# The first head's queries (and, in one layer, its pair's keys) computed ahead of the inverse transform in the second block

## What is computed

```python
def mla_queries(p, q_norm_g, w_uq, rope):
    cq = rms_norm(p[..., OFF_Q:OFF_KV], q_norm_g)
    q = (cq @ w_uq).reshape(B, L, MLA_HEADS, QK_NOPE + QK_ROPE)
    ...                                   # the last 32 channels of a head are rotated (rope)
def mla_attention(q_nope, q_rope, k_nope, k_rope, v):
    s = (jnp.einsum('bqhd,bkhd->bhqk', qn, k_nope) + jnp.einsum('bqhr,bkr->bhqk', qr, k_rope))
    prob = jax.nn.softmax(s.astype(jnp.float32) * scale, axis=-1).astype(v.dtype)
...
att_x = mla_attention(qn_x, qr_x, concat([kn_x, kn_c]), concat([kr_x, kr_c]), concat([v_x, v_c]))
x = x + g1 * heads_out(att_x, px, hy, w_out[l])      # attention, Fourier mix and hyena, side by side, by w_out
```

## The kernel before

| | values | back | first queries |
|---|---|---|---|
| layer 0 | v3 on 4, v4 on 5, v5 on 4 | c: 6 and 7 | 4, then 5, 6, 7 |
| layer 1 | v3 on 4, v4 on 5, v5 on 6 | x: 0 and 1 | 4, then 5 |

## Times and profile before

### The profile page before, as it was taken

How to read it: one execution, slowest core, us unless ns; L and a number is a source line. 1 busy time by engine, 2 the same in 40 slices (tenths; PEclk the granted TensorE clock), 3 DMA queues, 4 the chain that set the end, 5 groups by cost and what they waited for, 6 DMA issues and landing times.

```text
span 2508.6 us, 30040 instructions
## 1 busy us (share of the span) xinstructions
PE 2390.9 (95%) x11574; PEld 1858.9 (74%) x11574; DVE 1426.5 (57%) x2243; ACT 907.1 (36%) x1543; POOL 565.5 (23%) x431
## 2 busy tenths in 40 slices
PE   6999999999999997888999999999999989999998
PEld 5665667888877874667888888888775567788886
DVE  4465546888757436665475565544636674533435
ACT  4244444223244223675332221222421773423222
POOL 2523114223121213002131211211223002322221
PEclk9999899999999999999999999999999999999999
DMA  5411114555521311001144444331122112222321
GB/s 184 151 55 43 54 35 166 194 185 184 185 80 43 107 64 57 20 26 46 38 137 132 128 131 133 120 105 57 49 97 76 34 35 68 86 91 93 104 89 52
DMA packets 77913, 234.05 MB, mean 93 GB/s; under 512 B 9343, under 2 KB 12416, under 8 KB 77772
## 3 DMA queue, kind: packets, MB, share of 16 engines
q1 hardware_dynamic: 70928, 217.48, 26.4%
q0 software_dynamic: 3520, 11.58, 1.4%
q10 hardware_dynamic: 3324, 3.08, 0.4%
HBM read 224.20 MB, written 7.90 MB: 93 GB/s over the span
## 4 chain that ended last, share of the span: by engine, by line
PE 86%; DVE 7%; ACT 3%; issue 2%; POOL 2%; ACTq 0%; DVEq 0%; POOLq 0%
PE psum L652 35%; PE psum L923 24%; PE psum L691 4%; PE psum L1225 3%; PE psum L635 3%; PE psum L1256 2%; PE psum L1182 2%; PE psum L711 2%; PE psum L828 1%; PE psum L799 1%; PE psum L1240 1%; PE psum L577 1%; DVE mla_stat L2035 1%; PE psum L1196 1%; PE psum L846 1%
## 5 line engine op out<-in xcount | busy, mean ns | idle before, releaser
L652 PE MATMUL psum<-mix_split,weight_split 128*128 128x512 f32 (+1 forms) x3456 | 708.8, 366 | 1.3 <-POOL weight_split L2657 1.0
L652 PEld LDWEIGHTS psum<-mix_split,weight_split 128*128 128x128 f32 x3456 | 589.4, 188 | 117.4 <-POOL weight_split L2657 1.4
L923 PE MATMUL psum<-hidden,weight_split 128*128 128x512 f32 (+1 forms) x3072 | 629.5, 366 | 0.0
L923 PEld LDWEIGHTS psum<-hidden,weight_split 128*128 128x128 f32 x3072 | 523.7, 188 | 102.4
L2113 ACT CAST weight_split<-weight_ring 128x1024 fp32r<-128x1024 f32 x269 | 277.1, 1041 | 298.4 <-PE psum L923 231.6
L2657 POOL TENSOR_TENSOR weight_split<-weight_ring,weight_split 128x1024 fp32r<-128x1024 f32 x89 | 234.6, 2636 | 536.7 <-ACT weight_split L2113 536.2
L1681 DVE TENSOR_TENSOR hidden<-hidden_tmp,hidden 128x512 fp32r<-128x512 f32 (+1 forms) x128 | 157.1, 1247 | 313.8 <-POOL hidden_tmp L2790 313.8
L2790 POOL TENSOR_TENSOR hidden_tmp<-hidden_tmp 128x512 f32<-128x512 f32 (+1 forms) x128 | 126.3, 998 | 608.9 <-ACT hidden L2367 608.8
L1319 DVE TENSOR_TENSOR weight_split<-weight_ring,weight_split 128x1024 fp32r<-128x1024 f32 x180 | 228.5, 1272 | 51.7 <-ACT weight_split L2113 51.7
L2363 ACT ACTIVATE hidden_tmp<-psum 128x512 f32<-128x512 f32 (+1 forms) x128 | 69.2, 541 | 491.3 <-PE psum L652 491.3
L1698 DVE SCALAR_TENSOR_TENSOR residual<-psum,modulation,residual 128x512 f32<-128x512 f32 x192 | 120.0, 657 | 157.6 <-PE psum L923 157.6
(11 more groups left out here) (309 smaller groups left out, 2656.8 us busy)
## 6 DMA issues: line engine op xcount, KB each, us to landing
weight_ring<-in_w_mlp SPq DMA_DIRECT2D x128, 512.0 KB, 3.9
weight_ring<-in_w_ff SPq DMA_DIRECT2D x64, 512.0 KB, 4.8
mod_ring<-in_w_mod SPq DMA_DIRECT2D x48, 512.0 KB, 3.9
late_ring<-in_w_mod SPq DMA_DIRECT2D x96, 256.0 KB, 3.6
weight_ring<-in_w_in SPq DMA_DIRECT2D x45, 512.0 KB, 3.8
weight_ring<-in_w_out SPq DMA_DIRECT2D x24, 512.0 KB, 3.7
weight_ring<-in_tables SPq DMA_DIRECT2D x13, 512.0 KB, 3.6
weight_ring<-in_w_v SPq DMA_DIRECT2D x8, 512.0 KB, 4.3
```

The source lines that it names most:

```text
L652: m = pe.matmul(psum[:, b + r, 0:hi - lo], w[:, part_w, :], x[:, part_x, k, lo:hi], start=k == 0 and part_w + part_x == 0, stop=k == KT - ...
L923: mm = pe.matmul(psum[:, b + r, 0:hi - lo], w[:, part_w, :], G[:, part_x, f % (2 * GROUP), lo:hi], start=jj == 0 and part_w + part_x == 0, ...
```

## The change

`make_pair` on PE moves out of `attention_2` and becomes a generator that is begun in `mid`. A new helper `first_head` takes its first steps: in layer 0 four of them (queries of head 0 in two ranges, keys of the pair in two ranges), between values 5 and back c; in layer 1 one (queries of head 0), inside back x between f = 0 and f = 1. `attention_2` takes the rest; for the first pair the order is now queries, keys, queries, on all engines. Pairs 1 to 3 keep their order. On DVE the two products of the rotation (new helper `rope_products`) of head 0 go ahead of the convolution's last four instructions; the sum stays behind `hyena`. The last `back` of a layer takes its two banks from the pool "logits". ACT gets an activation of one column (exp of a constant, whose result nothing reads) ahead of its wait for `hyena`, and with it the load of its function table. The loads of w_uq and w_uk move ahead of the inverse table.

```diff
+            def make_pair(l, p):
+                tag, RG = f"mla{l}", ranges_of(l)
+                def queries(h, i):
...
+                i, i_k = use_load("w_uq", (l, p), 2 * 3 * P), use_load("w_uk", (l, p), 2 * P)
...
+                pe.wait_ge(*landed(i))
+                for part in (queries(2 * p, i), keys(), queries(2 * p + 1, i)) if p == 0 else (queries(2 * p, i), queries(2 * p + 1, i), keys()):
+                    yield from part
...
+                def first_head():
+                    pe.wait_ge(*when(f"qn{l}_vec", ("scaled", 2, len(RG) - 1)))
+                    first_pair[l] = make_pair(l, 0)
+                    for _ in range(1 if l else 4):
+                        next(first_pair[l])
                 def back(lo, hi, nm):
-                    b = take(2)
+                    b = take(2, "logits") if (lo, hi, nm) == streams[-1] else take(2)
                     for f in range(n):
+                        if l and f:
+                            first_head()
...
                     make_values([5])
+                    first_head()
                     back(*streams[1])
...
-                for _ in make_pair(0):
+                for _ in first_pair[l]:
                     pass
...  (vector_program)
+                    if (lo, hi, nm) == streams[-1]:
+                        rope_products(l, 0)
                     ve.wait_ge(*when("table", bank_of[tag, "back_load", nm]))
...  (scalar_program, attention_2)
+                ac.activation(rs[:, 0:1], vec("eps"), ACT.Exp).then_inc(*did("table_act", tag))
                 ac.wait_ge(*when(f"mid{l}_vec", ("hyena", streams_of(l)[-1][2], 1)))
```

More of the change, by code:

```diff
@@ L1171, in attention_2 @@
                 pe.wait_ge(*when(f"mid{l}_vec", ("v", 5)))
[L1173 to L1196, removed]
-                        m.then_inc(*did(tag + "_pe", ("k", p, r)))
-                        freed[b] = [(tag + "_act", ("k", p, r)), (tag + "_vec", ("k", p, r))]
-                        if r == 1:
-                            done_with[i] = (tag + "_pe", ("k", p, 1))
-                        yield
                 def logits(n):
@@ L2008, in make_pair, with keys @@
                             yield
[L2009 to L2015 removed]
+                    def keys():
+                        for r, (lo, hi) in enumerate(XB):
+                            h = 2 * p
+                            ve.wait_ge(*when(tag + "_pe", ("k", p, r)))
+                            if h > 2:
+                                ve.wait_ge(*when(tag + "_pe", ("logits", last_logits[h - 3])))
+                            ve.tensor_copy(KH[0:64, h % 3, lo:hi], psum[0:64, bank_of[tag, "k", p, r], 0:hi - lo]).then_inc(*did(tag + "_vec", ("k", p, r)))
+                            yield
+                    for part in (queries(2 * p), keys(), queries(2 * p + 1)) if p == 0 else (queries(2 * p), queries(2 * p + 1), keys()):
+                        yield from part
                 def feed(n):
@@ L2554, in make_pair, with keys @@
                             yield
-                    for r, (lo, hi) in enumerate(XB):
-                        h = 2 * p + 1
-                        ac.wait_ge(*when(tag + "_pe", ("k", p, r)))
-                        ac.wait_ge(*when(tag + "_vec", ("k", p, r)))
-                        if h > 2:
-                            ac.wait_ge(*when(tag + "_pe", ("logits", last_logits[h - 3])))
-                        ac.copy(KH[0:64, h % 3, lo:hi], psum[64:128, bank_of[tag, "k", p, r], 0:hi - lo]).then_inc(*did(tag + "_act", ("k", p, r)))
-                        yield
+                    def keys():
+                        for r, (lo, hi) in enumerate(XB):
+                            h = 2 * p + 1
+                            ac.wait_ge(*when(tag + "_pe", ("k", p, r)))
+                            ac.wait_ge(*when(tag + "_vec", ("k", p, r)))
+                            if h > 2:
+                                ac.wait_ge(*when(tag + "_pe", ("logits", last_logits[h - 3])))
+                            ac.copy(KH[0:64, h % 3, lo:hi], psum[64:128, bank_of[tag, "k", p, r], 0:hi - lo]).then_inc(*did(tag + "_act", ("k", p, r)))
+                            yield
+                    for part in (queries(2 * p), keys(), queries(2 * p + 1)) if p == 0 else (queries(2 * p), queries(2 * p + 1), keys()):
+                        yield from part
                 def feed(n):
```

55 lines of the change are left out of this document (37 added, 18 removed).

## The result

The changed kernel takes 2510.18 us (median of 20 runs, 2508.19 to 2514.2), the kernel before 2506.48 in the same comparison (20 runs, 2502.98 to 2511.09). The ratio is 1.0015, 95% interval 1.0010 to 1.0021: 3.7 us slower, inside what I called the same. The profiled execution took 2514.2 us with a span of 2512.4, against 2508.6 before, at the same mean clock of 0.981.

The account below looks back on a forecast made before the run. PE, busy 95% of the span, bounds the kernel, so moves pay only where it idles. Layer 0's -0.4 and layer 1's +3.3 sum to +2.9 us; from the median 2507.27 that gives 2510.2 us, range 2507.5 to 2512.3.

Parts of the forecast that it names:

- what I called the same: Whole kernel: differences below about 0.2%, 5.0 us, count as no change; chance of same 0.81.
- layer 0, queries start: Layer 0 on PE: moved queries wait for DVE's subtraction of value 5, start about 971.95; the gap stays.
- layer 0, convolution starts: Layer 0 on DVE: convolution follows back c's last start at 982.3 by 0.25, at 982.55.
- layer 0, logits: Layer 0, start of attention: first logits at 987.2, 0.4 us earlier.
- layer 1, back x starts: Layer 1 on PE: back x's first half waits for value 4's subtraction, starts 1932.1 after 7.3 us idle.
- layer 1, clock's cost behind the gap: Layer 1, back x and moved matmuls: lowered clock behind the gap costs 2.1 us.
- layer 1, first maximum: Layer 1, start of softmax: first logits 3.2 us later, another 0.1 from DVE's head 1 rotation, +3.3.
- layer 1, fall at the softmax: Layer 1, start of softmax: the likeliest case keeps the clock's fall, a loss of some 1.7 us.
- The step that failed: Layer 0 on PE: second head's queries end at 986.4, in time for logits at 987.2.
- the second rival: Layer 1, start of softmax: the clock's fall of some 1.7 us goes away; +1.2, 2508.5 us, chance 0.25.
- two terms that the prediction had at 0: Layer 0's attention and what follows it up to layer 1: no change in either, 0 us.
- The rival on the slower side: Layer 1's back x loses another 2.1 to the clock, layer 0's softmax start 1.7: +6.7, 2514.0 us, chance 0.13.

Follow-up runs that it names:

- The pool alone: Kernel before, only change: the last back stream alone draws its banks from the logits pool, nothing moved; 2511.36 us, ratio 1.0009.
- the free banks: Changed kernel, same order, with fixed free banks for first pair and last back: layer 0 2498.71 us, layer 1 2501.04, both 2491.66.
- other banks: Changed kernel with layer 0's second-head queries on banks 2 and 3 and first logits starting on bank 0; 2508.70 us, ratio 1.0006.
- before's second trace: Kernel before, profiled once more with no change; one run, span 2503.4 us.
- free banks in layer 1: Changed kernel with fixed free banks in layer 1 only, 2501.04 us, or in both layers, 2491.66 us.
- layer 1 alone: Changed kernel, but layer 0's queries and keys stay behind back c in the new first-pair order; 2506.27 us, ratio 0.9991.
- order alone: Kernel before with only the first pair reordered and the early table load, nothing moved ahead of back; 2508.91 us, run again 2509.97.
- layer 0 alone: Changed kernel, but layer 1's queries stay behind back x in the new first-pair order; 2509.69 us, ratio 1.0009.
- the two second traces: Kernel before and changed kernel, each profiled once more unedited; one run each, spans 2503.4 and 2506.5 us.
- both layers' banks: Changed kernel with fixed free banks in both layers for the first pair and last back; 2491.66 us, ratio 0.9939.

## Why the prediction came out right, step by step

| step | predicted | trace of the change |
|---|---|---|
| layer 0, queries start | 971.95 after 7.2 idle | 971.87 after 7.30, released by DVE's value 5 |
| layer 0, convolution starts | 982.55 | 982.64 |
| layer 0, logits | 987.2 (-0.4) | 989.13 (+1.5; L0 +1.24) |
| layer 1, back x starts | 1932.1 after 7.3 | 1932.1 after 7.11, less layer 0's shift |
| layer 1, clock's cost behind the gap | 2.1 | 2.7 (6.35 for 3.62) |
| layer 1, first maximum | +3.3 | +3.97 |
| layer 1, fall at the softmax | stays | gone, att -1.67 |
| sum | +2.9 | +3.7 timed, +3.8 span |

The mechanism held but for one wait: both gaps stay because the bank decides, and most of the loss is the first half of back x moved behind DVE's values. The pool alone shows that part by itself, and the free banks show that nothing else kept the gaps open.

**The step that failed** is "The second head's queries end on PE at 982.3 + 3.87 + 0.2 = 986.4, in time." I had followed the banks to the first moved matmul and to back, and not to the third user of the ring. Head 1's queries draw bank 4 again, which holds head 0's queries. Its last reader is ACT's copy (984.47 to 985.05), which waits for hyena, and hyena now comes after back c. So PE stood idle for 2.59 us, the queries ran until 989.3, and the first logits, next in PE's list, came at 989.13 instead of 987.2. With other banks the term is -0.5, as summed. The error is 1.6 to 1.8 us.

**Sizes.** The clock's cost in layer 1 was 0.6 short in this trace and 0.3 too high for the second (5.42 - 3.62 = 1.8); it varies over runs of the same kernel. On the other side 1.67 came back at the start of layer 1's softmax, which is the term of the second rival (1.7). But it is no clear gift of the change: before's second trace has no fall there, and has one of 1.7 later, between the 21st and 22nd maximum of layer 1; its L1 att is 131.00 all the same. Both traces of before have one fall in layer 1's attention up to there; the six traces with more than 7 us of idle time before back x have none, and neither have the two with free banks in layer 1, whose idle time is 0.5, nor layer 1 alone and the second trace of the order alone, whose idle time is 3.1 as before. That the fall went is shown; what decides it isn't. So +1.24, +3.97 and -1.67, with 0.2 from ahead of layer 0 and next to nothing between, add up to 3.8: the errors cancelled in part, 1.6 + 0.6 against 1.7.

**Luck.** The next to nothing between the layers is itself two terms that the prediction had at 0: layer 0's attention is 3.0 us longer in this trace, and what follows it 3.0 shorter. Between the two second traces the same stretch differs by 4.4. That the sum came within 1 us of the timed difference is luck as far as these terms go. That the 2510.2 of the prediction meets the 2510.18 measured is luck too: it started from the median of three runs, 2507.27, and over 20 runs before has 2506.48, so a start 0.8 too high made up for a change 0.8 too small. What the prediction got right is the two places that the change touches, but for the one wait named above.

**The rival on the slower side** did not come: its +6.7 needed more at half clock in both layers. The trace of layer 0 alone has a fall of 1.7 us near the start of layer 0's softmax, behind the 2.59 of idle time; that the whole of it can come in one run, no run shows.

## What to carry to other kernels

Work moved into an engine's idle time fills it only if its output buffer is free there. Write down for the changed order, buffer by buffer, who reads last and where that reader stands in its own engine's list, and go on until the ring has come round: the reader itself may wait for the work that was moved behind. Drawing one buffer from another pool shifts every later draw of the shared counter; here that alone cost as much in layer 1 as the whole change did there, and the same move with free banks gained 15 us.

## What the runs showed of the chip

- Work of PE behind an idle time of 7.1 to 7.4 us lost 1.7 to 2.7 us to the granted clock (8.73 for 7.06, 6.35 for 3.62). Behind 3.1 us it lost 1.5 (5.07 for 3.62, order alone, again) to 3.2 (layer 1 alone: 5.46 for 2.74 and 4.07 for 3.62). So the cost did not grow with the idle time. Behind the 0.5 and 0.9 us that free banks left, next to nothing was lost (3.69 for 3.62, 2.02 for 1.95). But a short idle time is no safeguard: in the kernel before four records of logits took 2.59 us behind 0.55, and 1.53 at the same place of its second trace.
- Inside the attentions the clock falls now and then, for a short time. The maxima of all kernels, counted from the first, agree within 0.5 us over more than a hundred us, but for steps at one or two tiles, most of them of 1.5 to 1.7 us. The kernel before had such a step in layer 1 at the fourth and fifth maximum in one trace and at the 22nd in the other, with sums equal to 0.1 us behind it, up to the 31st. A difference of 1.7 us between two traces may be such a step and says nothing yet of the change.
- An idle time pays twice when it is filled. With both layers' banks L0 and L1 fell by 9.3 + 5.3 = 14.6 us: the gaps give 7.35 - 0.94 and 3.08 - 0.51, 9.0 in all, the clock behind them 3.75 - 2.02 and 5.38 - 3.69, 3.4, and the shorter chain of the new order 1.33 + 1.04 = 2.4, which makes 14.8.
